# Feed-forward up-projections of a two-block model: 18 of 22 slabs a layer in seven products, one weight pair added by DMA, eight modulation tiles moved

## The reference

```python
for i in range(DEPTH):                                   # DEPTH = 4
    mod = c_act @ ada_w[i] + ada_b[i]                    # 1024 -> 6 * 1024
    sh1, sc1, g1, sh2, sc2, g2 = jnp.split(mod, 6, axis=-1)
    h = modulate(rmsnorm(x, mix_norm_g[i]), sh1, sc1)
    ...                                                  # mixer, x = x + (1 + g1) * y
    h = modulate(rmsnorm(x, ffn_norm_g[i]), sh2, sc2)
    x = x + (1.0 + g2)[:, None, :] * conv_ffn(h, ff_w_up[i], ff_conv_w[i], ff_conv_b[i], ff_w_down[i])

def conv_ffn(h, w_up, conv_w, conv_b, w_down):           # FF_DIM = 2816
    a = h @ w_up                                         # 1024 -> 2 * 2816
    pad = jnp.pad(a, ((0, 0), (CONV_W - 1, 0), (0, 0)))  # 3 causal taps per channel
    y = conv_b
    for j in range(CONV_W):
        y = y + conv_w[j] * pad[:, j:j + S, :]
    gate, val = jnp.split(y, 2, axis=-1)
    return (jax.nn.silu(gate) * val) @ w_down
```

## Time and profile before

| | |
|---|---|
| runs, median of 3 | 2770.34 us (2766.78 to 2773.43) |
| profiled execution, span from its first to its last instruction | 2768.3 us |
| profiled execution, time outside the span | not listed; the span lies 2.0 us under the median |
| PE busy | 2702.7 us, 98% |
| DVE busy | 1509.2 us, 55% |
| ACT busy | 490.3 us, 18% |
| POOL busy | 94.2 us, 3% |
| granted TensorE clock, mean | 0.997 of full speed |
| moved by DMA | 754.52 MB, 273 GB/s on the mean |

### The profile page before, as it was taken

How to read it: one execution, slowest core, us unless ns; L and a number is a source line. 1 busy time by engine, 2 the same in 40 slices (tenths; PEclk the granted TensorE clock), 3 DMA queues, 4 the chain that set the end, 5 groups by cost and what they waited for, 6 DMA issues and landing times.

```text
span 2768.3 us, 52705 instructions
## 1 busy us (share of the span) xinstructions
PE 2702.7 (98%) x22796; PEld 2148.6 (78%) x22796; DVE 1509.2 (55%) x3306; ACT 490.3 (18%) x1103; POOL 94.2 (3%) x180
## 2 busy tenths in 40 slices
PE   7999999999999999999999999999999999998987
PEld 6889998999998999999998899988335335742634
DVE  4549868797776886776776668665310111011001
ACT  3103305231223330212311300031101000100001
POOL 0110001100001000000000000000000000000000
PEclk9999999999999999999999999999999999999999
DMA  9776656765537667564444344456999999999996
GB/s 362 289 264 252 215 190 267 261 238 190 203 112 261 250 219 254 199 214 163 164 171 158 135 164 171 163 202 248 414 427 426 411 427 426 426 427 428 426 427 259
DMA packets 97522, 754.52 MB, mean 273 GB/s; under 512 B 10496, under 2 KB 12048, under 8 KB 42128
## 3 DMA queue, kind: packets, MB, share of 16 engines
q1 hardware_dynamic: 71920, 658.90, 61.2%
q0 software_dynamic: 25344, 92.29, 9.0%
q10 hardware_dynamic: 32, 0.02, 0.0%
HBM read 750.09 MB, written 1.06 MB: 271 GB/s over the span
## 4 chain that ended last, share of the span: by engine, by line
PE 87%; DMA 8%; DVE 3%; ACT 1%; issue 0%; SPq 0%; DVEq 0%; ACTq 0%
PE ps L864 16%; PE ps L1579 14%; PE ps L875 12%; PE ps L767 11%; PE ps L1616 7%; PE ps L946 3%; PE ps L1326 3%; PE ps L797 3%; DMA UW<-w_moe_up 2%; PE ps L964 2%; PE ps L844 2%; PE ps L1441 2%; PE ps L1246 2%; PE ps L777 2%; PE ps L1060 2%; DMA B<-w_moe_down 1%
## 5 line engine op out<-in xcount | busy, mean ns | idle before, releaser
L767 PE MATMUL ps<-HT,ring 128*128 128x256 f32 x1472 | 324.0, 379 | 0.0
L767 PEld LDWEIGHTS ps<-HT,ring 128*128 128x128 f32 x1472 | 277.4, 190 | 37.3 <-issue 1.0
L3223 DVE TENSOR_TENSOR C<-C,ps 128x256 f32<-128x256 f32 (+1 forms) x80 | 30.8, 388 | 364.3 <-ACT C L2095 364.3
L875 PE MATMUL ps<-A,UW 128*128 128x128 f32 x1224 | 161.7, 275 | 0.0
L875 PEld LDWEIGHTS ps<-A,UW 128*128 128x128 f32 x1224 | 149.0, 192 | 0.0
L1326 PE MATMUL ps<-HT,ring 128*128 128x256 f32 x640 | 142.5, 380 | 0.0
L3247 DVE TENSOR_TENSOR X<-X,ps 128x512 f32<-128x512 f32 x24 | 16.5, 688 | 218.2 <-PE ps L1538 217.6
L1326 PEld LDWEIGHTS ps<-HT,ring 128*128 128x128 f32 x640 | 120.3, 190 | 16.9 <-issue 1.2
L864 PE MATMUL ps<-A,ring 128*128 128x128 f32 x940 | 117.0, 275 | 0.0
L2095 ACT ACTIVATE C<-ps 128x256 f32<-128x256 f32 (+1 forms) x80 | 28.6, 358 | 478.9 <-PE ps L1579 478.9
L864 PEld LDWEIGHTS ps<-A,ring 128*128 128x128 f32 x940 | 111.3, 192 | 0.3
(11 more groups left out here) (580 smaller groups left out, 5003.4 us busy)
## 6 DMA issues: line engine op xcount, KB each, us to landing
ring<-w_ff_up SPq DMA_DIRECT2D x88, 1024.0 KB, 5.1
B<-w_moe_up SPq DMA_DIRECT2D x27, 2048.0 KB, 21.2
ring<-w_moe_up SPq DMA_DIRECT2D x26, 2048.0 KB, 21.7
B<-w_ada POOLq DMA_DIRECT2D x72, 512.0 KB, 6.1
ring<-w_ff_down SPq DMA_DIRECT2D x36, 1024.0 KB, 4.8
HT<-w_moe_up SPq DMA_DIRECT2D x16, 2048.0 KB, 22.5
ring<-w_moe_down SPq DMA_DIRECT2D x16, 2048.0 KB, 25.5
ring<-w_gm_in SPq DMA_DIRECT2D x30, 1024.0 KB, 6.3
```

The lines of the kernel that those rows point to most:

```text
L767: last = mm(bank[:, j * n:(j + 1) * n], ring[:, slot, k * 256 + j * P:k * 256 + j * P + P], src[:, k, :], start=(k == 0), stop=(k == KD - 1))
L875: last = mm(bank[:, at * P:(at + 1) * P], stationary[:, kind, k, :], moving(k), start=(start and k == 0), stop=(k == KD // 2 - 1), skip_gr ...
```

## The change

It does four things.

- `UP_SEVENS` is slabs 3 to 20 in each of the four layers: 18 seven-product slabs of 22.
- For each of them POOL issues a DMA (`add_pair`) that adds block 0 of the slab, read from HBM again (256 KB), to block 2 of the slab in the ring, once the slab has landed. Its semaphore is `pair_added[g % RING]`. Block 2 then holds the sum of blocks 0 and 2, which PE uses directly as one of the seven stationary operands, and DVE makes three sums instead of four (`sums_on_pair`), after a wait for that semaphore. The adds stand in POOL's order among the tile loads, by `PAIRS_BEFORE`; those of layer 3 stand at the end.
- A sum takes the place of a difference, so the value channels come out with their sign turned. `sums_of_values_negated` turns the matching sums of values, and the convolution's taps of these channels are negated once, in layer 0's mixer.
- Of the first 24 tiles, 12 are made in the up-projection (`UP_TILES`: steps 1, 2, 4, 6, 7, 9, 11, 12, 14, 16, 17, 19) and 12 in the down-projection (`DOWN_TILES`: beside the weight sums 2, 4, 5 and 7 two each, after sum 8 four), where there were 20 and 4.

```diff
-UP_SEVENS = {("sw_up", 0): range(3, KF), ("ff_up", DEPTH - 1): [m for m in range(3, 21) if m % 6 != 2]}
-for layer in range(DEPTH - 1):
-    UP_SEVENS["ff_up", layer] = [m for m in range(3, 21) if m % 3 != 2]
+UP_SEVENS = {("sw_up", 0): range(3, KF)}
+for layer in range(DEPTH):
+    UP_SEVENS["ff_up", layer] = range(3, KF - 1)
...
+UP_TILES = [m for m in range(1, KF - 1) if m % 5 in (1, 2, 4)]
+DOWN_TILES = {2: 2, 4: 2, 5: 2, 7: 2, 8: 4}
+PAIR = KD // 2 * P
...
+STEP_OF = {t: (UP_TILES[t - ADA_DEEP] if t - ADA_DEEP < len(UP_TILES) else KF) for t in range(ADA_DEEP, ADA_MIXER)}
+PAIRS_BEFORE = {t: range(3 if t == ADA_DEEP else min(STEP_OF[t - 1] + 4, KF), min(STEP_OF[t] + 4, KF)) for t in STEP_OF}
...
         def _(pool):
+            def add_pair(layer, m):
+                g = first_slab["ff_up", layer] + m
+                pool.wait_ge(w_ready[g % RING], 16 * (g // RING))
+                pool.dma_start(ring[:, g % RING, 2 * PAIR:3 * PAIR], ins["w_ff_up"][layer * KF + m, :, 0:PAIR],
+                               accum_op=ALU.add).then_inc(pair_added[g % RING], 16)
...
                 layer, t = divmod(n, ADA_TILES)
+                if layer and ADA_DEEP <= t < ADA_MIXER:
+                    for m in PAIRS_BEFORE[t]:
+                        if m in UP_SEVENS["ff_up", layer - 1]:
+                            add_pair(layer - 1, m)
...
                 pool.dma_start(buf, ins["w_ada"][n]).then_inc(ready, 16)
+            for m in UP_SEVENS["ff_up", DEPTH - 1]:
+                add_pair(DEPTH - 1, m)
...
-                product(y, 1, sums, 2, lambda k: summed(2, k), True).then_inc(part_done.tick(), 1)
+                product(y, 1, w, 2, lambda k: summed(2, k), True).then_inc(part_done.tick(), 1)
...
+            def sums_on_pair(layer, m, sums):
+                g = first_slab["ff_up", layer] + m
+                dve.wait_ge(pair_added[g % RING], 16 * additions(first_slab, layer, m))
+                w = seven_w(g)
+                step(tt(sums[:, 1], w[:, 2], w[:, 3], ALU.add))
+                tt(sums[:, 0], sums[:, 1], w[:, 0], ALU.subtract)
+                tt(sums[:, 3], w[:, 1], sums[:, 1], ALU.add).then_inc(weights_summed.tick(), 1)
...
+                    for layer in range(DEPTH):
+                        for lo, hi in runs(UP_SEVENS["ff_up", layer]):
+                            taps = conv[:, layer, lo:hi, 1, 0:3]
+                            negated = ts(taps, taps, -1.0, None, ALU.mult)
+                    step(negated)
...
-                    if i + 1 < DEPTH and 0 < m < KF - 1:
-                        ada_next(n + m - 1)
+                    if i + 1 < DEPTH and m in UP_TILES:
+                        ada_next(n + UP_TILES.index(m))
...
+                    for k in ((1, 2, 3, 4), (5, 6, 7), (8,), ())[m]:
+                        if i + 1 < DEPTH and k in DOWN_TILES and k in (4, 7):
+                            down_tiles(k)
                         weight_sums(("ff_down", i), k)
+                        if i + 1 < DEPTH and k in DOWN_TILES and k not in (4, 7):
+                            down_tiles(k)
+                    if i + 1 < DEPTH and m == 2:
+                        ada_bias(n, n + ADA_MIXER)
```

More of the change, by code:

```diff
@@ L200, with runs @@
 GM_SEVENS = range(3, GM_GROUPS + 1)
+UP_TILES = [m for m in range(1, KF - 1) if m % 5 in (1, 2, 4)]
+DOWN_TILES = {2: 2, 4: 2, 5: 2, 7: 2, 8: 4}
+PAIR = KD // 2 * P
+def runs(numbers):
+    edges = [m for m in numbers if m - 1 not in numbers]
+    return [(lo, next(m for m in range(lo, KF + 1) if m not in numbers)) for lo in edges]
+STEP_OF = {t: (UP_TILES[t - ADA_DEEP] if t - ADA_DEEP < len(UP_TILES) else KF) for t in range(ADA_DEEP, ADA_MIXER)}
+PAIRS_BEFORE = {t: range(3 if t == ADA_DEEP else min(STEP_OF[t - 1] + 4, KF), min(STEP_OF[t] + 4, KF)) for t in STEP_OF}
 def up_banks(m):
@@ L208, in fold_banks, with additions @@
     return FOLD_PAIRS[m % 3] if m > 2 else (m, None)
+def additions(first_slab, layer, m):
+    g = first_slab["ff_up", layer] + m
+    return sum((first_slab["ff_up", i] + k) % RING == g % RING and (i, k) <= (layer, m)
+               for i in range(DEPTH) for k in UP_SEVENS["ff_up", i])
 def fold_frees(layer):
@@ L378, in build @@
         weights_summed = Count(sem("weights_summed"))
+        pair_added = [sem(f"pair_added{b}") for b in range(RING)]
         values_summed = Count(sem("values_summed"))
@@ L2197, in sums_of_values, with sums_of_values_negated @@
                 tt(t[:, 3], a[:, :, 1, 0, :], t[:, 1], ALU.subtract).then_inc(values_summed.tick(), 1)
+            def sums_of_values_negated(a, t):
+                tt(t[:, 0], a[:, :, 0, 0, :], a[:, :, 0, 1, :], ALU.subtract)
+                step(tt(t[:, 2], a[:, :, 1, 1, :], a[:, :, 0, 1, :], ALU.subtract))
+                step(stt(out=t[:, 1], in0=t[:, 0], scalar=-1.0, in1=a[:, :, 1, 1, :], op0=ALU.mult, op1=ALU.subtract))
+                stt(out=t[:, 3], in0=t[:, 1], scalar=-1.0, in1=a[:, :, 1, 0, :], op0=ALU.mult, op1=ALU.subtract)\
+                    .then_inc(values_summed.tick(), 1)
             def value_sums(part, made):
@@ L2646, in ffn, with down_tiles @@
                 value_sums(2, made)
+                def down_tiles(k):
+                    at = n + len(UP_TILES) + sum(count for other, count in DOWN_TILES.items() if other < k)
+                    for t in range(at, at + DOWN_TILES[k]):
+                        ada_next(t)
                 def between(m):
[L2650 to L2656, removed]
+                    for k in ((1, 2, 3, 4), (5, 6, 7), (8,), ())[m]:
+                        if i + 1 < DEPTH and k in DOWN_TILES and k in (4, 7):
+                            down_tiles(k)
                         weight_sums(("ff_down", i), k)
+                        if i + 1 < DEPTH and k in DOWN_TILES and k not in (4, 7):
+                            down_tiles(k)
+                    if i + 1 < DEPTH and m == 2:
+                        ada_bias(n, n + ADA_MIXER)
                     if i == 0 and m == 3:
```

10 lines of the change are left out of this document (8 added, 2 removed).

## The result

The changed kernel takes **2775.7 us** (median of 11 runs, 2772.9 to 2782.9) against 2768.7 us for the kernel before in the same comparison (11 runs). The ratio is 1.0026, with a 95% interval of 1.0018 to 1.0033: slower by 0.26%, where 0.46% faster was forecast. The profiled execution of the changed kernel has a span of 2781.1 us and is the slowest of its 11 runs (2782.9 us), so its losses are somewhat larger than usual; a second profile stands among the experiments.

A forecast was written before the change was run, and what follows sets the result against it. PE's own work was taken to bound the up-projection. PE's -13.8 us and +1.0 us for first adds take the span from 2768.3 to 2755.5 us, forecast as a 2757.5 us median; range 2754 to 2786 us.

The forecast's parts named there:

- PE's term: Up-projections: 21 more slabs become seven-product slabs, each 0.66 us shorter on PE; -13.8 us in all.
- DVE in the up-projection: Three weight sums keep DVE's steps under 6.25 us; value sums make it 2.5 us late, within 4.4 us to spare; nothing.
- the negated taps: Layer 0's mixer: four small DVE operations fit where DVE idles 3.48 us for ACT; cost nothing.
- the down-projection: Eight moved tiles, 9.8 us of DVE, fit 12.35 us of its idle time there; cost nothing.
- The first add of a layer: Up-projection start, slab 3: the add behind eight tile loads lands late, 0.3 us taken three times; +1 us.
- The added wait: Up-projection: DVE waits for adds queued behind tile loads, some tenths of a microsecond, PE not at all; no loss.
- A: Landing time of an add behind a tile load in the up-projection; taken as 6.4 us, whole gain eaten at 7.15 us.
- 27 x (A - 6.2) - 13: PE's loss in us in up-projections of layers 0 to 2 for longer landings, less about 13 us of slack; begins at 6.7 us.
- The rule of the Trainium skill: DMA adds need two source reads, half a copy's rate; up-projection adds would land in 6.9 us, time 6 us higher.
- The one on the other side: Slow adds make DVE PE's bound in up-projections of layers 0 to 2, landing beyond 7.15 us; 2798 us at 8.2; chance 0.27.
- The add is somewhat late: Up-projection adds land in 6.75 to 7.35 us, half to all the gain eaten; 2759 to 2775 us; chance 0.15.
- Four sums would do: Up-projection: the adds save DVE work that did not bind; dismissed as over 6.25 us a step on average; no chance.

The follow-up runs named there:

- second profile: The changed kernel, with no further edit, profiled again: 2779.1 us in a single run (the kernel before 2768.9).
- experiment 1: Changed kernel without its 72 adds and DVE's waits for them; seven products, three sums and moved tiles stay: 2859.3 us, ratio 1.0328.
- (7): Kernel before with only the eight tiles per layer moved from the up-projection to the down-projection: ratio 1.0002.
- experiment 5: Changed kernel with its 72 adding transfers as plain copies, same place in the queue: 2764.0 us in one run.
- experiment 4: Changed kernel with each add a step earlier and each layer's first add ahead of the last four of eight tile loads: 2756.0 us, ratio 0.9961.

## Why the prediction was wrong, by its steps

- **PE's term, -13.8 us: right.** Layer 3 took 133.28 us where 133.2 was forecast; so did all layers without adds.
- **DVE in the up-projection, the negated taps, the down-projection, all nothing: right.** Without adds DVE never made PE wait in the up-projection (experiment 1); its 4.3 us of slack, and 1.95 behind the value sums, are the 4.4 and 4.4 - 2.5 us of the prediction. The moved tiles cost nothing (7), and PE is unbroken in the down-projection.
- **"The first add of a layer", +1 us: wrong, and the largest error.** The eight tile loads drained as the step had it: in layer 1 the last, issued at 504.1 us, landed 15.5 us later, 11.8 us after slab 1 began (11.7 us by the earlier trace rows). But the step let the add follow within 0.6 to 1.3 us, 2.6 at the far end, as if the engines then had nothing else. It landed at 523.4 us, 3.7 us behind the last tile (2.9 us in layer 0), and in between the engines were full, at 407 GB/s and a share of 1.00 from 519 to 521 us, where the earlier trace rows show them nearly empty at the same point. The load of slab 5 and the add for slab 4 were on their way then too; which of them held the engines was not separated. DVE waited 5.7 us and PE 3 us. One more cost stood in no term: the lower clock after PE's pause, 1.7 and 3.0 us in layers 0 and 1. Slab 3 lost 12.9 us in the three layers, and moving this one add gained 13 us.
- **"The added wait", no loss: wrong, by its slack more than by A.** The median landing was 6.8 us in the first profile, of which the formula 27 x (A - 6.2) - 13 would make 3 us, and 6.4 in the second, just as taken, of which it would make nothing. Behind slab 3, PE lost 10.9 and 9.0 us; moving the adds a step sooner, with the first one left late, gained 8 us. What failed is the 4.4 us a layer (the 13 of the formula) that were to stand against the adds. The prediction's own step before spends 2.5 of them on the value sums in steps 9 and 17, and 1.95 us are left there (experiment 1). In the changed kernel the adds had taken DVE's lead down to about 1 us at slab 11 of each layer, the value sums took 2.3 more, and PE stood at slab 12. At slab 20 the same happened in layers 0 and 2. Nor can DVE make up much of what it has lost: a round of 6.2 us of landing and 6.3 us of DVE and POOL is PE's 12.5 us, and nothing over. The rest of the term holds: 18 of the 19 mid-stage waits in layers 0 to 2 were for adds issued right behind a tile load, and at 5.0 us of landing (experiment 5) the loop costs next to nothing. It also took one figure for A, where adds behind the first of a layer took 4.6 to 8.9 us in layers 0 to 2, and 5.1 us for the slab loads, which rose to 6.3 us beside the adds.
- **The rule of the Trainium skill** ("Collectives: The Full Stack", the section on the fold count and ReduceScatter): the estimate of A by it, 6.9 us, is near the 6.8 us of the first profile and above the 6.4 of the second. The time worked out from it, 6 us above my sum, was still 12 us too low, since the formula counted a slack that was partly spent and the first add stood outside it.
- **The rivals.** The one on the other side named the mechanism, DVE held by a late add in layers 0 to 2, but put its start at 7.15 us of landing; PE's loss began below that, because part of the slack was spent on value sums, and more than half of it came from the first add, for which the prediction has a term of its own. "The add is somewhat late" has the 6.8 us of the first profile in its range and 2775 us as its upper end, next to the 2775.7 measured, but by its formula 6.8 us make 2761 us: the time agrees by luck. (Its 6.75 to 7.35 us make 1.9 to 18 us, not half to all of the gain.) "Four sums would do" was given no chance: they do cost 2.8 us a layer, as that rival's sum said, but DVE's 18 slabs with four sums still beat the kernel before.

The forecast of 2757.5 us is about what the change is worth with its adds well placed: 2756.0 us in experiment 4, for another order of POOL than the one that was forecast.

## What to carry to other kernels

A transfer added to a queue is priced by when it can be issued, so list for each one what stands ahead of it in its issuer's program: here the wait for a tile's buffer and eight loads issued at once cost 18 us, and reordering POOL's list returned it. Price the first pass of a stage by itself, behind all that is issued at the stage's start. Spend a slack only once: take off what other steps of the same engine use, at the place where they use it. And where a step closes a loop through two queues, compare the length of one round with what the bound engine needs for it, not a mean landing with a margin.

## What the runs showed of the hardware

- An adding DMA of 256 KB took 1.72 us of the 16 engines, the plain copy 0.80 us; it landed in 6.8 us (6.4 in the second profile) instead of 5.0, and its issue on POOL took 867 ns instead of 538.
- PE's pauses of 2.2 to 3.0 us at the start of the stage (five of them, in three profiles) were followed by 3 to 7 us at half the granted clock; one of 2.24 us in experiment 5 and those of 1.75 us and less were not.
- In the changed kernel, slab loads of the up-projections rose from 5.1 to 6.3 us and tile loads from 6.1 to 6.6 us at the median (6.0 and 6.3 us in the second profile).
